# Hybrid conv and gMLP trunk on 8 cores: the 31-tap convolution over eight phases and 16 channels in place of four and 32

## The chip, the cores and the metric

The kernel runs on the 8 cores of one Trainium2 chip. Each core computes its own two sequences of 2048 tokens (4096 rows of 1024 channels); nothing passes between cores. The metric is the device time of one execution, in microseconds (us), of the slowest core.

## What is computed

Layer 0 is a convolution mixer and a squared-ReLU MLP, layer 1 a gMLP mixer and another MLP, with an RMSNorm ahead of each part and at the end. The change is in layer 0's mixer A and around it:

```python
z = h @ w_in  # (B, S, IN_EVEN)
a_val, a_gate, b_gate, c_gate, b_val = jnp.split(
    z, [A_DIM, 2 * A_DIM, 2 * A_DIM + B_DIM, 2 * A_DIM + 2 * B_DIM], axis=-1)
# A: GLU -> causal depthwise conv (31) -> LayerNorm over channels -> swish
a = a_val * jax.nn.sigmoid(a_gate)
a = causal_depthwise_conv(a, conv_a_w) + conv_a_b
a = jax.nn.silu(layer_norm(a, ln_a_g, ln_a_b))
# B: B * conv3(C * h)
bo = b_gate * causal_depthwise_conv(c_gate * b_val, conv_b_w)
return jnp.concatenate([a, bo], axis=-1) @ w_out  # shared pointwise output projection
```

A_DIM and B_DIM are 512. The gMLP mixer (layer 1) ends in `y @ w_out`, whose order of tiles the change touches too.

## The kernel before

**Macro tiles.** A core's 4096 tokens are four macro tiles (`mt`) of 1024 tokens. Each passes through mixer 0 (`Mixer0`), MLP 0, mixer 1 (`mixer1`), MLP 1 and the final norm. In a macro tile, token blocks `tb` are 128 tokens, halves `hf` are 512. Big products are groups of 8 matmuls of 128x512 (`fm_group`, `tm_group`, line L550). Eight PSUM banks are handed out in turn (`next_bank`); a bank is written again only when its reader is done with it.

**Order.** There is no scheduler. The kernel is written out by hand in one order; every engine executes its own instructions in that order, and `Prog` puts a semaphore wait where data or a buffer needs it. So an instruction that waits holds all that stands behind it on its engine. SP issues the loads of `x`, the stores of `y` and the DMAs that move data between partitions; GpSimd (POOL) issues the weight loads (a ring of five 1 MB slots, `issue`, `issue_quarter`; in the prologue by quarters).

**The convolution.** Time is split into phases: position t of a 1024-token tile is in phase t mod 4. After the gate (`glu`, which writes `aP`), 32 DMAs (`to_x`, L717) bring the 512 channels into `X`, whose 128 partitions are 4 phases x 32 channels, with 16 channel groups of 256 columns and 8 columns of history. The depthwise convolution is then a banded 128x128 matrix for each of 9 column shifts: `conv(m, pr)` (L793) is 2 groups x 9 matmuls of 256 columns, and there are 8 calls for each macro tile, 32 in all. The scalar engine (ACT) evicts each group twice (with bias L802, squared L805); `sums` adds up for the LayerNorm over channels (DVE and POOL), `stat_mm` (L830) sums over partitions with one fp32 matmul of 512 columns (two passes on TensorE), `ln_var`, `ln_rstd`, `ln_norm` (L849) normalise on DVE, `silu` (L854) is on ACT, 16 DMAs (`to_mix`, L859) bring the result back to channels on partitions (`mixA`), and eight small copies on DVE (`reorder`, L864) put it in the order of tokens in `mixTA`. `out` is the output projection; its first four groups (7 of 8 matmuls each) need the reorders of half 0 and branch B without its last quarter.

**Branch B** (`b_branch`): two products and a gate multiply for each half (`b_cv`), five tap operations on DVE (`b_taps`), two more products and multiplies (`b_gates`): 6 groups of 8 matmuls for each of 4 channel quarters m.

**Where it lies.** For macro tiles 2 and 3 the projections and branch B run ahead (`ahead`) before MLP 1 of the tile before, and the convolution, LayerNorm and `to_mix` are hung into that MLP (`behind`: keys (quarter of the MLP, 0 for the first product or 1 for the second, place in it)). Macro tile 1 uses `behind` too. Macro tile 0 has no such cover: its mixer is in the prologue, interleaved with the `glu` and branch B of tile 1 (`m1`). There, `stat_mm` of tile 0 stands in the fifth pair of `m1.glu`, the silus and `to_mix` in branch B quarters 0 and 1, the reorders of half 0 ahead of the taps of quarter 3, then `out` of tile 0. The norm of tile 1's input (`pre`: `load` by SP, `stat` on ACT and then two small POOL operations, `xn` on ACT, `tr` on TensorE and DVE) is also interleaved.

**Names in the trace.** Buffers of the arena (`X`, `aP`, `a_conv`, `mixA`, `cw` and others) all show as `arena`.

## Time and profile before

| | us |
|---|---|
| median of 3 runs | 2687.58 |
| lowest and highest run | 2686.13, 3231.77 |
| the profiled execution, its own time | 2687.07 |
| its span (slowest core, core 0) | 2685.5 |
| span of the fastest core (core 1) | 2673.3 |
| TensorE busy (core 0) | 2638.5 (98%) |
| VectorE, ScalarE, GpSimd busy | 1035.9, 879.4, 942.3 |

The median and the profiled execution belong to the same level; the highest run stands apart and nothing is compared with it. Engines are called PE (TensorE matmul), PEld (its weight loads), DVE (VectorE), ACT (ScalarE), POOL (GpSimd) and SP (the queue that issues DMAs). A row of the trace over time gives start, duration, engine, source line, operation, tiles, count, and in brackets the idle time ahead of it with what ended it. Since a PE row's duration includes the tail of its last matmul, the pace of matmuls is read from one row's start to the next row's start.

### The profile page before, as it was taken

Reading aid. Unit: us, or ns where it says so; the run is one execution under the profiler, and the core shown is the slowest. Engines: PE = TensorE matmul, PEld = TensorE weight load, DVE = VectorE, ACT = ScalarE, POOL = GpSimd, SP = SyncE. Lnnn points to the kernel's source line nnn. Section 1 sums busy time; section 2 is a strip of 40 time slices with the busy share of each in tenths; the row PEclk is TensorE's granted clock in tenths of the full one; section 3 lists DMA queues with packets and bytes.
Section 4 is the critical chain, followed back from the end, with each engine's and each line's share of the span. In section 5 each row is a group of like instructions: output and inputs, shape, how many; then the busy total and the mean of one; then the engine's idle time right before and its main releaser. Section 6 shows DMA issues by size and latency. Waiting matters only on the chain.

```text
span 2685.5 us, 39687 instructions; the slowest of 8 cores (2673.3 to 2685.5 us)
## 1 busy us (share of the span) xinstructions
PE 2638.5 (98%) x13400; PEld 1260.9 (47%) x13400; DVE 1035.9 (39%) x1582; ACT 879.4 (33%) x1487; POOL 942.3 (35%) x1229
## 2 busy tenths in 40 slices
PE   6999999999999999999999999999999999999998
PEld 3544444455444444445544444444554444444443
DVE  3564223732543115743245212655233512273223
ACT  2433115432333235412234223632223421354112
POOL 3214223333433342403453434142344333325223
PEclk9999999999999999999999999999999999999999
DMA  9426334455575533345558544155455834325432
GB/s 203 113 55 117 73 66 77 77 100 98 95 184 130 118 72 64 66 95 96 101 116 227 95 95 88 39 95 104 87 101 107 213 68 92 64 44 101 77 63 79
DMA packets 57908, 265.28 MB, mean 99 GB/s; under 512 B 8176, under 2 KB 16368, under 8 KB 33904
## 3 DMA queue, kind: packets, MB, share of 16 engines
q0 software_dynamic: 29664, 202.39, 42.0%
q1 hardware_dynamic: 28048, 60.37, 7.1%
q8 instruction: 112, 1.84, 0.3%
q14 instruction: 84, 0.69, 0.1%
HBM read 439.67 MB, written 17.04 MB: 170 GB/s over the span
## 4 chain that ended last, share of the span: by engine, by line
PE 95%; DMA 3%; DVE 1%; issue 1%; POOL 0%; ACT 0%; DVEq 0%; SPq 0%; POOLq 0%; ACTq 0%
PE bank L550 90%; PE bank L793 2%; PE bank L431 2%; DMA ring<-od_w_out 2%; DMA h<-x 0%; DMA arena<-x 0%; DVE arena L1022 0%; PE bank L1016 0%; DVE arena L970 0%; ACT junk L406 0%; PE bank L830 0%; DVE st L986 0%; DVE xnT L434 0%; DVE arena L995 0%; DMA y<-arena 0%
## 5 line engine op out<-in xcount | busy, mean ns | idle before, releaser
L550 PE MATMUL bank<-xnT,ring 128*128 128x512 bf16 x5888 | 1297.4, 380 | 9.5 <-ACT arena L634 5.8
L550 PE MATMUL bank<-ring,arena 128*128 128x512 bf16 x5120 | 1125.2, 379 | 5.4 <-DMA ring<-od_w_out 5.4
L572 DVE TENSOR_TENSOR h<-bank,h 128x512 f32<-128x512 f32 x640 | 440.7, 691 | 1303.8 <-PE bank L550 1263.2
L550 PEld LDWEIGHTS bank<-xnT,ring 128*128 128x128 bf16 x5888 | 574.2, 98 | 689.1 <-issue 21.9
L550 PEld LDWEIGHTS bank<-ring,arena 128*128 128x128 bf16 x5120 | 498.6, 98 | 594.2 <-issue 9.4
L600 POOL TENSOR_TENSOR arena<-arena 128x512 bf16<-128x512 f32 x512 | 551.4, 1083 | 313.8 <-ACT arena L598 313.6
L598 ACT ACTIVATE arena<-bank 128x512 f32<-128x512 f32 x512 | 303.7, 597 | 974.5 <-PE bank L550 930.5
L351 POOL DMA_DIRECT2D ring<-w x128 | 72.5, 567 | 453.7 <-PE bank L550 452.7
L406 ACT ACTIVATE junk<-h 128x1024 bf16<-128x1024 f32 x135 | 142.0, 1052 | 197.0 <-DVE h L572 178.8
L434 DVE TENSOR_TENSOR xnT<-bank,sm 128x1024 bf16<-128x1024 bf16 x128 | 155.2, 1217 | 50.6 <-PE bank L431 50.4
L408 POOL TENSOR_SCALAR st<-st 128x1 f32<-128x1 f32 x159 | 36.0, 227 | 372.2 <-ACT junk L406 370.3
L416 ACT ACTIVATE xn_tm<-h,st 128x1024 bf16<-128x1024 f32 x96 | 109.5, 1147 | 103.2 <-POOL st L410 103.2
L550 PE MATMUL bank<-ring,xnT 128*128 128x512 bf16 x512 | 115.7, 379 | 0.0
L410 POOL TENSOR_TENSOR st<-st,mhalf 128x1 f32<-128x1 f32 x159 | 92.6, 582 | 23.6 <-POOL st L408 0.3
L813 POOL TENSOR_TENSOR arena<-arena 128x512 f32<-128x512 f32 x16 | 20.3, 1268 | 224.1 <-ACT arena L805 224.1
L634 ACT ACTIVATE arena<-bank 128x512 f32<-128x512 f32 x64 | 38.1, 597 | 181.0 <-PE bank L550 148.6
L802 ACT ACTIVATE arena<-bank,sm 128x256 f32<-128x256 f32 x64 | 30.4, 474 | 201.2 <-PE bank L793 194.5
L635 DVE TENSOR_TENSOR arena<-bank,arena 128x512 bf16<-128x512 f32 (+1 forms) x64 | 44.2, 691 | 131.4 <-PE bank L550 100.6
L1022 DVE SCALAR_TENSOR_TENSOR arena<-bank,sm,biasT 128x128 f32<-128x128 f32 x256 | 86.0, 349 | 20.4 <-DVE arena L1022 0.5
L431 PE MATMUL bank<-ident,xn_tm 128*128 128x128 bf16 x896 | 68.9, 222 | 18.7 <-DVE xn_tm L1115 18.7
L431 PEld LDWEIGHTS bank<-ident,xn_tm 128*128 128x128 bf16 x896 | 59.8, 99 | 43.4 <-issue 19.5
L550 PEld LDWEIGHTS bank<-ring,xnT 128*128 128x128 bf16 x512 | 49.9, 98 | 59.5
(82 smaller groups left out, 1000.0 us busy)
## 6 DMA issues: line engine op xcount, KB each, us to landing
ring<-w POOLq DMA_DIRECT2D x128, 1024.0 KB, 10.4
arena<-convw POOLq DMA_DIRECT2D x16, 1152.0 KB, 11.9
h<-x SPq DMA_DIRECT2D x32, 512.0 KB, 6.7
ring<-od_w_in POOLq DMA_DIRECT2D x16, 1024.0 KB, 9.0
y<-arena SPq DMA_DIRECT2D x31, 512.0 KB, 4.3
arena<-x SPq DMA_DIRECT2D x24, 512.0 KB, 10.4
ring<-ev_w_in POOLq DMA_DIRECT2D x10, 1024.0 KB, 14.3
ring<-ev_w_out POOLq DMA_DIRECT2D x8, 1024.0 KB, 12.2
```

The costliest lines, as they stand in the source:

```text
L351: op("pool", lambda e: e.dma_start(out=ring[s][:], in_=W[wn][c]), [], wkeys(s), dma=f"w{s}")
L406: op("act", lambda e: e.activation(out=junk[:], in_=src, func=AF.Square, scale=1.0 / 32, accum_out=scol(c)), keys, [("st", c), ("junk",)])
L410: op("pool", lambda e: e.tensor_tensor(out=scol(c), in0=scol(c), in1=mhalf[:], op=ALU.pow), [("st", c), ("mhalf",)], [("st", c)])
L416: op("act", lambda e: e.activation(out=dst, in_=src, func=AF.Copy, scale=scol(c)), keys + [("st", c)], [dkey])
L431: r = e.transpose(tbk[:, kc * 128:(kc + 1) * 128], xa[:, kc * 128:(kc + 1) * 128], ident[:])
L434: op("dve", lambda e: e.tensor_tensor(out=xnT[:, :, tb * 128:(tb + 1) * 128], in0=tbk.rearrange("p (k n) -> p k n", k=8), in1=sm[:, SM_G + ...
L550: r = e.matmul(banks[b][:], lhsT=lhs(kc), rhs=rhs(kc), start=start and n == 0, stop=stop and n == len(kcs) - 1)
L572: op("dve", lambda e: e.tensor_tensor(out=h[:, tb, d * 512:(d + 1) * 512], in0=banks[b][:], in1=h[:, tb, d * 512:(d + 1) * 512], op=ALU.ad ...
L598: op("act", lambda e, b=b, rb=rb: e.activation(out=rbuf[rb], in_=banks[b][:], func=AF.Relu), [("ps", b)], [(f"rbuf{rb}",)])
L600: op("pool", lambda e, rb=rb, c=j * 4 + m, s=s, hq=hq: e.tensor_tensor(out=hq[:, c, s * 512:(s + 1) * 512], in0=rbuf[rb], in1=rbuf[rb], op ...
L793: r = e.matmul(banks[b][:, gi * 256:(gi + 1) * 256], lhsT=cw[wk][:, i, q, :], rhs=self.X[:, 4 * m + i, q:q + 256], start=(q == 0), stop=(q ...
L1022: op("dve", lambda e, b=b, j=j, g=g: e.scalar_tensor_tensor(out=svb[k][:, g, :], in0=banks[b][:, j * 128:(j + 1) * 128], scalar=sm[:, SM_L ...
```

## The change

It has these parts.

1. Eight phases of 16 channels: position t is in phase t mod 8. `X` has 32 groups of 128 columns with 4 columns of history, the band needs 5 shifts, and a `conv(c, pr)` call is 4 groups x 5 matmuls of 128 columns. `c` runs over four chunks of 8 groups. Weights of the convolution are 128 x 5120 for each chunk in place of 128 x 4608. Each call is evicted by 8 ACT operations of 128 columns in place of 4 of 256.
2. `to_x` is 4 x 16 DMAs in place of 2 x 16, `to_mix` 4 x 16 in place of 16, each over 16 partitions in place of 32. The reorders wait for all of `to_mix`.
3. `stat_mm` multiplies 256 columns in place of 512; `sums` folds on DVE and POOL.
4. `behind`: statistics, silus and `to_mix` earlier in the MLP (in quarter 2's first product, chunk by chunk), the reorders later.
5. `mixer1`: the output projection takes output half 0 of token blocks 0 to 2 first, then half 1 of them.
6. Prologue of tile 0: the first weight quarters are issued after the first statistic, blocks 4 and 5 are normalised earlier, four loads of tile 1's input come in the glu; `to_x` follows the glu; two of its chunks are issued after branch B quarter 1; `conv` of chunk 1 comes after branch B quarter 2; the statistics of `pre` for blocks 4 to 7 stand in `last_b` as pairs with their `xn`; `stat_mm` comes two glu pairs later; the silus and `to_mix` come within quarter 0 of tile 1's branch B; all eight reorders come after branch B.

The core of the diff (layout of the arena, packing of the inputs on the host and the same slicing in branch B are left out):

```diff
-            def to_x(self, pr):
+            def to_x(self, c):
+
                 def move(e, k):
-                    i, s = k // 4, k % 4
-                    return e.dma_start(
-                        out=self.X[32 * s:32 * s + 32].rearrange("p (m i) n -> p m i n", i=4)[:, 2 * pr:2 * pr + 2, i, 8:264],
-                        in_=aP[32 * i:32 * i + 32, 2 * pr:2 * pr + 2, s, :])
-                op("sp", move, [("aP", m, hf) for m in (2 * pr, 2 * pr + 1) for hf in range(2)], [(self.kX, pr)],
-                   dma=f"X{pr}", n=16)
+                    i, p = 2 * c + k // 8, k % 8
+                    return e.dma_start(out=self.X[16 * p:16 * p + 16, 4 * i:4 * i + 4, 4:132],
+                                       in_=aP[16 * i:16 * i + 16, :, p, :])
+                op("sp", move, [("aP", m, hf) for m in range(4) for hf in range(2)], [(self.kX, c)], dma=f"X{c}", n=16)
...
-            def conv(self, m, pr):
-                wk = m % 2 if self.mt == 0 else 0
...
+            def conv(self, c, pr):
...
+                wk = c % 2 if self.mt == 0 else 0
...
                 def go(e):
-                    for gi in range(2):
-                        i = pr * 2 + gi
-                        for q in range(9):
-                            r = e.matmul(banks[b][:, gi * 256:(gi + 1) * 256], lhsT=cw[wk][:, i, q, :],
-                                         rhs=self.X[:, 4 * m + i, q:q + 256], start=(q == 0), stop=(q == 8))
+                    for gi in range(4):
+                        for q in range(5):
+                            r = e.matmul(banks[b][:, gi * 128:(gi + 1) * 128], lhsT=cw[wk][:, 4 * pr + gi, q, :],
+                                         rhs=self.X[:, 8 * c + 4 * pr + gi, q:q + 128], start=(q == 0), stop=(q == 4))
                     return r
...
-                op("pe", lambda e: e.matmul(banks[b][:], lhsT=blk[:], rhs=part, start=True, stop=True),
-                   [("part", 0), ("part", 1), ("blk",)], [("ps", b)])
+                op("pe", lambda e: e.matmul(banks[b][:, 0:256], lhsT=blk[:], rhs=part_b, start=True, stop=True),
+                   [("part", "b", 0), ("part", "b", 1), ("blk",)], [("ps", b)])
...
-            def to_mix(self):
-                op("sp", lambda e, k: e.dma_start(out=mixA[32 * (k // 4):32 * (k // 4) + 32, k % 4],
-                                                  in_=self.sgate[32 * (k % 4):32 * (k % 4) + 32, k // 4]),
-                   [(self.kS, g) for g in range(16)], [("mixA",)], dma="mx", n=16)
+                    out=self.sgate[:, g, :], in_=a_conv[:, g, :], func=AF.Silu, bias=sm[:, SM_LNB + g:SM_LNB + g + 1],
+                    scale=sm[:, SM_LNG + g:SM_LNG + g + 1]), [ak(g), ("sm",)], [(self.kS, g)])
+
+            def to_mix(self, c):
+                def move(e, k):
+                    i, p = 2 * c + k // 8, k % 8
+                    return e.dma_start(out=self.mixA[16 * i:16 * i + 16, p], in_=self.sgate[16 * p:16 * p + 16, 4 * i:4 * i + 4, :])
+                op("sp", move, [(self.kS, g) for g in range(8 * c, 8 * c + 8)], [(self.kM, c)], dma=f"mx{c}", n=16)
 
...
-                    in_=half_cols(mixA[:, :, m], hf)), [("mixA",)], [(self.kA, m, hf)])
+                    out=self.mixTA[:, m, hf * 512:(hf + 1) * 512].rearrange("p (b s n) -> p s b n", b=4, s=8),
+                    in_=half_cols(self.mixA[:, :, m], hf)), [(self.kM, c) for c in range(4)], [(self.kA, m, hf)])
...
                 for t in range(4, 8):
+                    if t in late:
+                        nm.stat(t)
                     nm.xn(t)
...
-                self.glu({5: [lambda: self.to_x(0)], 7: [lambda: self.to_x(1)]})
+                self.x_halo()
+                self.glu()
+                for c in range(4):
+                    self.to_x(c)
...
-                self.save_halo()
+                side.setdefault((0, 0, 10), []).append(self.save_halo)
...
-                for m in range(4):
-                    fq, t0 = m // 2, (0, 6)[m % 2]
-                    add((fq, 1, t0), self.conv, m, 0)
-                    add((fq, 1, t0 + 1), self.conv, m, 1)
-                    if m < 3:
-                        add((fq, 1, t0 + 1), load_cw, self.mt, m + 1)
-                add((2, 0, 4), self.stat_mm)
-                add((2, 0, 4), self.ln_var)
-                add((2, 0, 6), self.ln_rstd)
-                for m in range(4):
-                    add((2, 0, 7 + 2 * m), self.ln_norm, m)
-                for g in range(16):
-                    add((2, 1, g // 2), self.silu, g)
-                add((2, 1, 7), self.to_mix)
+                for c, (k0, k1) in enumerate((((0, 1, 0), (0, 1, 1)), ((0, 1, 6), (0, 1, 7)),
+                                              ((1, 0, 12), (1, 0, 13)), ((1, 1, 4), (1, 1, 5)))):
+                    add(k0, self.conv, c, 0)
+                    add(k1, self.conv, c, 1)
+                    if c < 3:
+                        add(k1, load_cw, self.mt, c + 1)
+                add((2, 0, 1), self.stat_mm)
+                add((2, 0, 1), self.ln_var)
+                add((2, 0, 2), self.ln_rstd)
+                for c in range(4):
+                    add((2, 0, 3 + 3 * c), self.ln_norm, c)
+                    for i in range(8):
+                        add((2, 0, min(16, 5 + 3 * c + i // 4)), self.silu, 8 * c + i)
+                    add((2, 0, min(16, 6 + 3 * c)), self.to_mix, c)
                 for m in range(4):
                     for hf in range(2):
-                        add((3, 0, 6 + 2 * m + hf), self.reorder, m, hf, "dve")
+                        add((3, 0, 10 + m + hf), self.reorder, m, hf, "dve")
...
-            for tb in range(NTB):
-                for d in range(2):
...
-                post(tb)
+            order = [(tb, d) for d in range(2) for tb in range(3)] + [(tb, d) for tb in range(3, NTB) for d in range(2)]
+            for tb, d in order:
...
+                if d == 1:
+                    post(tb)
...
-        more_weights(2)
...
-        for tb in range(4, NTB):
-            load_h(0, tb, [("w", 0, 0), ("w", 1, 0)])
...
-            if tb < 3:
-                more_weights(2)
+            more_weights(2)
+            if tb == 0:
...
-        nm.stat(4)
-        first_xn(4)
+        for tb in (4, 5):
+            nm.stat(tb)
+            first_xn(tb)
         more_weights(3)
...
-        m0.glu({2: [lambda: pre.load(0, [("aP", 2, 0)]), lambda: pre.load(1)],
-                5: [lambda: m0.to_x(0)], 7: [lambda: m0.to_x(1)]})
-        prologue_spatial()
...
+        m0.glu({0: [first_tr(4), more_x(6, 3, 0)], 1: [first_tr(5), more_x(7, 3, 1)],
+                2: [first_tr(6), lambda: more_weights(3), lambda: [pre.load(t, [("aP", 2, 0)] if t == 0 else ()) for t in range(4)]],
+                5: [prologue_spatial]},
+               {3: [first_tr(7)]})
+        m0.x_halo()
+        m0.to_x(0)
+        m0.to_x(1)
...
-            pre.load(tb + 4)
+        for tb in (2, 3):
+            pre.stat(tb)
+            pre.xn(tb)
+        for tb in range(4, 8):
+            pre.load(tb)
+        m0.to_x(2)
+        m0.to_x(3)
         prologue_bias()
         m0.conv(0, 0)
...
+        m0.b_branch(2)
         m0.conv(1, 0)
         m0.conv(1, 1)
         load_cw(0, 3)
...
-        m0.b_branch(2)
-        for tb in (2, 3, 4, 5):
-            pre.stat(tb)
-        for tb in (2, 3):
...
+        rest = m0.last_b(pre, (4, 5, 6, 7))
         m1.weights(m0)
         m1.glu({0: [rest[0], lambda: m0.conv(2, 0)], 1: rest[1:] + [lambda: m0.conv(2, 1)],
-                2: [lambda: m0.conv(3, 0)], 3: [lambda: m0.conv(3, 1)],
-                4: [m0.stat_mm, m0.ln_var], 5: [m0.ln_rstd, lambda: m0.ln_norm(0)],
-                6: [lambda: m0.ln_norm(1)], 7: [lambda: m0.ln_norm(2)]})
+                3: [lambda: m0.conv(3, 0)], 4: [lambda: m0.conv(3, 1), m0.save_halo],
+                6: [m0.stat_mm, m0.ln_var], 7: [m0.ln_rstd, lambda: m0.ln_norm(0)]})
...
+        m0.ln_norm(1)
         m1.b_halo(0)
         m1.b_cv(0, 0)
         silus(0)
+        m0.ln_norm(2)
         m1.b_cv(0, 1)
         silus(1)
         m1.b_taps(0)
+        m0.ln_norm(3)
+        silus(2)
         m1.b_gates(0)
-        m0.ln_norm(3)
-        m1.b_halo(1)
-        m1.b_cv(1, 0)
-        silus(2)
-        m1.b_cv(1, 1)
         silus(3)
...
-        m0.to_mix()
-        for pr in range(2):
-            m1.to_x(pr)
-        m1.b_taps(1)
-        m1.b_gates(1)
+        for c in range(4):
+            m0.to_mix(c)
+        for c in range(4):
+            m1.to_x(c)
+        m1.x_halo()
+        m1.b_branch(1)
...
-        for m in range(4):
-            m0.reorder(m, 0, "dve")
         m1.b_taps(3)
         m1.b_gates(3)
         m1.free_in()
         for m in range(4):
-            m0.reorder(m, 1, "dve")
+            for hf in range(2):
+                m0.reorder(m, hf, "dve")
```

How this moves instructions, at the three places that matter later. First SP, at the end of the prologue (L859 before and L878 after are `to_mix` of tile 0, L717 and L728 are `to_x` of tile 1, L1227 and L1237 the load of `b_v`). Before:

```order
L859 DMA arena<-arena 32x1024 [waits s_act_0,s_dve_0]
L859 DMA arena<-arena 32x1024 x15
L717 DMA arena<-arena 32x2x256 [waits d_cb_0,s_pe_0]
L717 DMA arena<-arena 32x2x256 x31
L1227 DMA arena<-bigc 128x1024 [waits d_mx_0,d_mx_1,s_dve_0]
```

After:

```order
L878 DMA arena<-arena 16x512 [waits s_act_0,s_dve_0]
L878 DMA arena<-arena 16x512 x31
L878 DMA arena<-arena 16x512 [waits s_act_0]
L878 DMA arena<-arena 16x512 x15
L878 DMA arena<-arena 16x512 [waits s_act_0]
L878 DMA arena<-arena 16x512 x15
L728 DMA arena<-arena 16x4x128 [waits d_cb_0,s_pe_0]
L728 DMA arena<-arena 16x4x128 x63
```

Tile 0's way back is 64 DMAs on this queue where it was 16, each with half the partitions and half the elements of a partition; the first 32 of them wait for the silus of the first two chunks (the 32 share one wait).

Second DVE, at the end of tile 1's branch B (L864 and L882 are `reorder`, L755 to L759 and L764 to L768 the taps of quarter 3, L768 and L777 the last multiplies, L572 and L577 the sum into `h` behind `out`'s matmuls). Before:

```order
L635 TENSOR_TENSOR arena<-bank3,arena 128x4x128 [waits s_pe_0,s_act_0,s_pool_0]
L864 COPY arena<-arena 128x4x4x32 [waits d_mx_0,d_mx_1,d_cw1_0]
L864 COPY arena<-arena 128x4x4x32 x3
L755 TENSOR_SCALAR arena<-arena,sm 128x1024 [waits s_pool_0,s_dve_0]
...
L768 TENSOR_TENSOR arena<-bank4,arena 128x4x4x32 [waits s_pe_0,s_dve_0]
L768 TENSOR_TENSOR arena<-bank5,arena 128x4x4x32 [waits s_pe_0]
L864 COPY arena<-arena 128x4x4x32 x4
L572 TENSOR_TENSOR h<-bank6,h 128x512 [waits s_pe_0]
```

After:

```order
L640 TENSOR_TENSOR arena<-bank3,arena 128x8x64 [waits s_pe_0,s_act_0,s_pool_0]
L764 TENSOR_SCALAR arena<-arena,sm 128x1024 [waits s_pool_0,s_dve_0]
...
L777 TENSOR_TENSOR arena<-bank4,arena 128x8x4x16 [waits s_pe_0,s_dve_0]
L777 TENSOR_TENSOR arena<-bank5,arena 128x8x4x16 [waits s_pe_0]
L882 COPY arena<-arena 128x8x4x16 [waits d_mx0_0,d_mx0_1,d_mx1_0,d_mx1_1,d_mx2_0,d_mx2_1,d_mx3_0,d_mx3_1,d_cw1_0]
L882 COPY arena<-arena 128x8x4x16 x7
L577 TENSOR_TENSOR h<-bank6,h 128x512 [waits s_pe_0]
```

The four copies of half 0 that stood ahead of the taps now stand behind the last multiplies, with the wait for all four chunks of `to_mix`.

Third ACT, around `last_b` of tile 0 (L406 and L411 are `stat`, L416 and L421 `xn`, L634 and L639 the evictions of gates). Before:

```order
L406 ACTIVATE junk,st<-arena 128x1024 [waits d_st2_0,s_act_0]
L406 ACTIVATE junk,st<-arena 128x1024 [waits d_st3_0,s_act_0]
L634 ACTIVATE arena<-bank0 128x512 [waits s_pe_0,s_dve_0]
L634 ACTIVATE arena<-bank5 128x512 [waits s_pe_0,s_dve_0]
L416 ACTIVATE xn_tm0<-arena,st 128x1024 [waits s_pool_0]
L416 ACTIVATE xn_tm1<-arena,st 128x1024 [waits s_pool_0]
L416 ACTIVATE xn_tm2<-arena,st 128x1024 [waits s_pool_0,s_pe_0]
L416 ACTIVATE xn_tm3<-arena,st 128x1024 [waits s_pool_0,s_pe_0]
```

After:

```order
L639 ACTIVATE arena<-bank0 128x512 [waits s_pe_0,s_act_0,s_dve_0]
L639 ACTIVATE arena<-bank5 128x512 [waits s_pe_0,s_act_0,s_dve_0]
L411 ACTIVATE junk,st<-arena 128x1024 [waits d_st0_0]
L421 ACTIVATE xn_tm0<-arena,st 128x1024 [waits s_pool_0]
L411 ACTIVATE junk,st<-arena 128x1024 [waits d_st1_0,s_act_0]
L421 ACTIVATE xn_tm1<-arena,st 128x1024 [waits s_pool_0]
L411 ACTIVATE junk,st<-arena 128x1024 [waits d_st2_0,s_act_0]
L421 ACTIVATE xn_tm2<-arena,st 128x1024 [waits s_pool_0,s_pe_0]
```

The statistics that waited for loads ahead of the two gate evictions now stand behind them, each followed by the `xn` that needs POOL's answer to it.

## Rows read from the trace of the kernel before

**Rows 1.** The page, busy time, share of the span and instructions: PE.

```profile
PE 2638.5 (98%) x13400; PEld 1260.9 (47%) x13400; DVE 1035.9 (39%) x1582; ACT 879.4 (33%) x1487; POOL 942.3 (35%) x1229
```

**Rows 2.** Instructions over time, PE, a convolution call between two products.

```profile
582.20 2.14 PE L793 MATMUL bank<-arena 128*128 128x256 bf16 x18
584.17 3.62 PE L550 MATMUL bank<-ring,arena 128*128 128x512 bf16 x16
```

**Rows 3.** The same view: sixteen transposes of 128 columns.

```profile
106.41 1.06 PE L431 MATMUL bank<-ident,xn_tm 128*128 128x128 bf16 x16
107.30 1.89 PE L550 MATMUL bank<-xnT,ring 128*128 128x512 bf16 x8
```

**Rows 4.** Groups by line and form, PEld: busy us, mean ns, idle before.

```profile
L793 PEld LDWEIGHTS bank<-arena 128*128 128x128 bf16 x576 | 55.8, 97 | 12.2
```

**Rows 5.** Instructions over time, PE: the statistics' matmul and what follows.

```profile
150.52 1.10 PE L830 MATMUL bank<-arena,blk 128*128 128x512 f32 x2 [1.50 <-POOL arena L819]
151.45 51.96 PE L550 MATMUL bank<-xnT,ring 128*128 128x512 bf16 x240
```

**Rows 6.** PE over time: waits at mixer 1's output projection.

```profile
521.65 12.25 PE L550 MATMUL bank<-ring,arena 128*128 128x512 bf16 x56 [1.90 <-DMA ring<-od_w_out]
...
1105.93 1.89 PE L550 MATMUL bank<-ring,arena 128*128 128x512 bf16 x8 [0.66 <-DMA ring<-od_w_out]
...
1762.92 1.89 PE L550 MATMUL bank<-ring,arena 128*128 128x512 bf16 x8 [0.73 <-DMA ring<-od_w_out]
...
2421.26 13.93 PE L550 MATMUL bank<-ring,arena 128*128 128x512 bf16 x56 [2.09 <-DMA ring<-od_w_out]
```

**Rows 7.** Spans and granted clock of the cores.

```profile
core 0: 2685.5 us, clock 0.996
core 1: 2673.3 us, clock 0.997
```

**Rows 8.** PE over time in the prologue: waits for inputs and for ACT.

```profile
23.74 9.66 PE L550 MATMUL bank<-xnT,ring 128*128 128x512 bf16 x32 [1.48 <-DVE xnT L434]
...
44.98 36.38 PE L550 MATMUL bank<-xnT,ring 128*128 128x512 bf16 x160 [2.25 <-DVE xnT L434]
...
115.84 9.69 PE L550 MATMUL bank<-xnT,ring 128*128 128x512 bf16 x32 [5.76 <-ACT arena L634]
```

**Rows 9.** All engines over time, 100 to 117 us: ACT and POOL there.

```profile
111.74 1.06 ACT L406 ACTIVATE junk<-arena 128x1024 bf16<-128x1024 f32 x1 [7.76 <-DMA arena<-x]
...
115.03 0.19 ACT L406 ACTIVATION_READ_ACCUMULATOR junk<-arena 128x1 f32 x1
115.12 1.06 ACT L634 ACTIVATE arena<-bank 128x512 f32<-128x512 f32 x2
...
115.74 0.57 POOL L410 TENSOR_TENSOR st<-st,mhalf 128x1 f32<-128x1 f32 x1
...
116.08 1.15 ACT L416 ACTIVATE xn_tm<-arena,st 128x1024 bf16<-128x1024 f32 x1
```

**Rows 10.** The issues on SP's queue over time: start, us for all.

```profile
54.67 23.80 SPq L717 DMA_DIRECT2D arena<-arena  x32
...
80.86 1.73 SPq L650 DMA_DIRECT2D wsT_bf<-ws_scr  x4
...
180.41 10.06 SPq L859 DMA_DIRECT2D arena<-arena  x16
190.62 21.99 SPq L717 DMA_DIRECT2D arena<-arena  x32
```

**Rows 11.** DMA issues, 150 to 212 us: size, median us to landing.

```profile
arena<-arena SPq DMA_DIRECT2D x16, 64.0 KB, 2.0
```

**Rows 12.** All engines over time, 150 to 222 us: silus, reorders, `out`.

```profile
168.28 2.06 ACT L854 ACTIVATE arena<-arena,sm 128x256 bf16<-128x256 f32 x4
...
200.82 0.89 DVE L864 COPY arena<-arena 128x512 bf16<-128x512 bf16 x4
...
203.25 13.98 PE L550 MATMUL bank<-ring,arena 128*128 128x512 bf16 x64
...
205.90 1.29 DVE L768 TENSOR_TENSOR arena<-bank,arena 128x512 bf16<-128x512 f32 x2
```

286 lines of the change are left out of this document (141 added, 145 removed).

## The prediction

> **What bounds the kernel now.** I read the page first. PE is busy 98% of the span [rows 1], so time is won only by fewer PE columns or by removing PE waits; a faster DVE, ACT or POOL is worth nothing where PE does not wait for it. Then PE over time: from about 150 us on it runs in one piece, with four short waits for the output weights of mixer 1 [rows 6]. All other PE idle time lies in the prologue (tile 0), where there is no MLP to hide anything [rows 5, 8]. So there are two questions: what PE work goes, and what the new order does to PE's waits in the prologue. The pace of a full product: 240 matmuls of 512 columns start at 151.45 and the next piece at 203.25 [rows 5, 12], 51.8 / 240 = 0.216 us each, 1.727 us for a group of 8.
>
> **The convolution.** A call of 18 matmuls of 256 columns takes 584.17 - 582.20 = 1.97 us [rows 2]. The new call has 20 matmuls of 128 columns. The nearest row with that shape and a new weight load for each matmul is the transposes: 16 in 107.30 - 106.41 = 0.89 us, 0.0556 us each [rows 3]. So 20 x 0.0556 = 1.11 us, 0.86 us less, and 32 calls give 27.5 us. Bounds: a weight load shows 97 ns for one [rows 4]; if each of the 20 were paid in full, a call would be 1.94 us and nothing would be won. The 16 transposes have the same loads and speak against it, so I take 0.0556.
>
> The Trainium skill (TensorE: Matmul & The Clock Gate, Back-to-back issue gap) gives about 81 ns as the sustained spacing of 128-column matmuls with weight loads. The row shows 55.6 ns over 16 of them; by the page a call would be 1.62 us and the 32 calls would give 11.2 us.
>
> **Smaller PE terms.** The statistics' matmul takes 151.45 - 150.52 = 0.93 us [rows 5]; half the columns, half of that, four times: 1.9 us. The 1.50 us that PE waited ahead of it in tile 0 [rows 5] goes, since a second glu pair (3.45 us) now stands between the last convolution and it: 1.5 us.
>
> **Mixer 1's output weights.** PE waits 1.90 + 0.66 + 0.73 + 2.09 = 5.4 us for the second of two weight tiles [rows 6]. The new order does two more groups (3.45 us) of the first tile before it needs the second; each wait is shorter than that. The fourth wait was also followed by a slower stretch: the same 56 matmuls take 13.93 in place of 12.25 us [rows 6], 1.7 us. Together 7.1 us. These waits are those of core 0; the fastest core ends 12.2 us earlier [rows 7], so the slowest cores gain here and come nearer to the others.
>
> **Start of the prologue.** PE's losses that show: waits of 1.48 and 2.25 us, and slow stretches after them (32 matmuls in 9.69 us where 32 x 0.216 plus a tail of 0.16 is 7.1; 160 in 36.38 where it would be 34.7) [rows 8], 8 us together. The first weight quarters now leave DMA room for the first inputs, but themselves come later, and blocks 4 to 7 have to wait for them. The same bytes have to arrive, so I count a little under half: 3.5 us won. Bounds: 8 us won; 5 us lost if the quarters come late by most of the time they are now issued later.
>
> **Around `last_b`.** Before, ACT waited 7.76 us for a staged load, with gate evictions behind it [rows 9]; PE lost 5.76 us and then 2.6 us in a slow stretch [rows 8]. The loads are now early, and the evictions stand ahead. But the four statistics now each have their `xn` right behind: 1.06 + 0.19 us, then POOL's answer about 1.1 us later (115.22 to 116.31), then 1.15 us [rows 9]: 3.5 us a pair, 14 us for four, and the first gate eviction of `m1.glu` is queued behind them. Counted from `last_b`'s start, ACT is free of them at about 22.4 us and evicts by 23.0; PE comes to the bank again at about 20.5. So 2.5 us of waiting, some 4 us more while DVE (taps, multiplies, transposes) catches up, and 2.6 us of slow clock: about what goes. I count 0. Bounds: 8.4 us won, 4 us lost.
>
> **The way back of tile 0.** This is where the change costs. Count from the end of the statistics' matmul. PE now has one glu pair and 24 groups of branch B before `out`: 26 x 1.727 = 44.9 us (before 30 groups, 51.8). The first `to_mix` waits for the first half of the silus; before, that half ended at 168.28 + 2.06 = 170.3 [rows 12], 18.9 us after the statistics [rows 5]. The chain of table loads and normalisation is the same and two pairs fewer lie in between: I take 17. SP then issues 64 DMAs. A `to_mix` DMA costs SP 10.06 / 16 = 0.63 us, and `to_x` 21.99 / 32 = 0.69 us, with half the bytes and twice the pieces [rows 10]: the price is for one DMA, not for its size. So 64 x 0.63 = 40.3 us, the last lands 2.0 us later [rows 11]: 59.3. The reorders wait for all of it, and `out` needs seven of the eight at 0.89 / 4 = 0.22 us [rows 12]: 60.9. PE waits 60.9 - 44.9 = 16.0 us, and after such a wait pays a slow stretch as above, 2.6 us: 18.6 us lost. Before, half of the reorders were done at 201.7, ahead of `out` at 203.25 [rows 12], with only 16 DMAs. Lower bound: even with all data there, the reorders now stand behind the last multiplies, which end at 207.19 less the 0.89 of the copies that moved, 3.1 us after PE gets to `out`, plus 1.6: 4.6 us. Upper bound: 19 us to the silus and 23.80 / 32 = 0.74 us a DMA, as when weights stream beside it [rows 10]: 27.7 us.
>
> **Hidden.** In tiles 1 to 3 the same 64 and 64 DMAs have room: `to_x` 64 x 0.69 = 44 us against branch B and MLP product of over 69 us (40 groups) ahead of the first convolution; `to_mix` 40 us against 36 groups (62 us) between the first chunk and the reorders. The doubled count of evictions (8 of 128 columns for 4 of 256) is on ACT, whose share is 33% [rows 1], under products; if that cover failed, 64 more operations of some 0.25 us a tile would be 16 us.
>
> **Sum.** 27.5 + 1.9 + 1.5 + 7.1 + 3.5 = 41.5 us won, 18.6 lost: 22.9 us. The profiled execution's span is 2685.5 us, so 2662.6; its own time is 2687.07, half a microsecond under the median of 2687.58, so the median would be 2664.7: I say **2665**.
>
> **The rivals.**
> - A, SP is quicker with half-width DMAs. The four DMAs into `wsT_bf` took 1.73 / 4 = 0.43 us each [rows 10]. Then `to_mix` is in time and only the lower bound of 4.6 us remains: 41.5 - 4.6 = 36.9, so 2651. For it: that row. Against: those have DRAM on one side, the two kinds from SBUF to SBUF cost 0.63 and 0.69.
> - B, the prologue's start wins nothing and loses 3 us, because the first weights come later: 2671. For it: the first product needs two quarters which are now issued behind the first statistic.
> - C, weight loads bound the short matmuls at 81 ns: 16.3 us less won, 2681. Against it: rows 3. The Trainium skill's page above is the source of that spacing; no row here shows it.
> - D, the other side: SP's issue slows to 1.2 us, since each DMA has smaller pieces and the weight loads of `out` and MLP 0 compete. The wait at `out` is 17 + 64p + 3.6 - 44.9, with 2.6 of clock 64p - 21.7; at p = 1.2 it is 55.1 us, net 13.6 lost, 2701. It decides from p = 0.99 us on. Against it: 0.74 us is the slowest row [rows 10].
> - E, everything goes well (A, `last_b` and the start at their bounds): 2687.6 - 36.9 - 8.4 - 4.5 = 2638.
>
> **How the numbers follow.** Forecast 0.48, A 0.22, B 0.13, C 0.07, D 0.05, E 0.05. The range reaches from A to B with some room for their own terms: 2646 to 2677, leaving out C, D and E. A difference of 2% (54 us) is about what a measurement of this kernel can tell from no change: faster than 2634 needs more than E, 0.03; slower than 2741 needs D and more, 0.02; within 2%, 0.95.
>
> **What would show it.** A convolution call between two products takes 1.11 us. PE shows one wait of some 16 us at `out` of tile 0, ended by the reorders, and these waited for a DMA; SP's 64 issues take 40 us. No wait for `od_w_out`. PE's first product starts earlier than 23.7 us. A wait of 2 to 3 us, ended by ACT's gate eviction, follows `last_b`. The forecast is wrong if a call takes 1.6 us or more, if SP takes 0.45 us or 1 us a DMA, or if new waits show in tiles 1 to 3.

## The result and the profile after

The forecast was 2665 us in a range of 2646 to 2677. Measured were 2705.5 us (2705.75 and 2705.27) against 2687.58: 1.007 of the time before, 95% interval 1.0041 to 1.01. So the change costs some 0.7% where 0.8% was to be won. The forecast, its range and its sign are wrong; "within 2%" holds. Every time given here and below is a median of those executions in which no four cores of the chip were slowed down together by a much lower granted clock.

Cores 0 and 1 took 2685.5 and 2673.3 us before [rows 7]; they and all others are later now, and core 6 ends 9 to 19 us behind cores 0 to 5.

The kernel after, spans and mean granted clock of the cores:

```profile
core 0: 2693.8 us, clock 0.989
core 1: 2688.8 us, clock 0.990
...
core 5: 2684.8 us, clock 0.990
core 6: 2704.1 us, clock 0.981
core 7: 2696.4 us, clock 0.982
```

I compare core 0 with core 0, since the rows before are of that core, and come back to cores 6 and 7 below. The kernel after, PE over time on core 0 (start us, busy us, ..., in brackets the idle time ahead of the row and what ended it):

```profile
19.22 5.00 PE L555 MATMUL bank<-xnT,ring 128*128 128x512 bf16 x16 [1.48 <-DVE xnT L439]
29.66 1.01 PE L436 MATMUL bank<-ident,xn_tm 128*128 128x128 bf16 x8 [5.45 <-DVE xn_tm L1133]
...
77.60 1.95 PE L666 MATMUL bank<-arena 128*128 128x128 f32 x16
88.74 4.42 PE L801 MATMUL bank<-arena 128*128 128x128 bf16 x40 [9.19 <-DMA arena<-arena]
92.96 10.91 PE L555 MATMUL bank<-xnT,ring 128*128 128x512 bf16 x48
108.66 4.43 PE L801 MATMUL bank<-arena 128*128 128x128 bf16 x40 [4.80 <-DMA arena<-arena]
112.88 6.00 PE L555 MATMUL bank<-xnT,ring 128*128 128x512 bf16 x24
118.72 1.06 PE L436 MATMUL bank<-ident,xn_tm 128*128 128x128 bf16 x16
...
129.59 1.29 PE L801 MATMUL bank<-arena 128*128 128x128 bf16 x20
130.72 3.62 PE L555 MATMUL bank<-xnT,ring 128*128 128x512 bf16 x16
138.53 1.01 PE L436 MATMUL bank<-ident,xn_tm 128*128 128x128 bf16 x8 [4.20 <-ACT arena L639]
140.23 2.29 PE L801 MATMUL bank<-arena 128*128 128x128 bf16 x20 [0.69 <-DVE arena L640]
...
166.24 0.59 PE L847 MATMUL bank<-arena,blk 128*128 128x256 f32 x2
166.67 45.06 PE L555 MATMUL bank<-xnT,ring 128*128 128x512 bf16 x208
237.52 15.43 PE L555 MATMUL bank<-ring,arena 128*128 128x512 bf16 x64 [25.79 <-DVE arena L882]
```

The first bracket with a DMA is new and stood nowhere in the prediction: PE waits 9.19 and 4.80 us for X ahead of convolution chunks 0 and 1. The last is the forecast wait at `out`, but 25.79 us long and not 16. Behind 237.52 PE has one wait left on this core, 1.37 us at 617.39 for convolution weights, and none on the others. (A call of the convolution is the row at 129.59; the transposes at 118.72 are those of `last_b`.) The core's way, cut at the same points of the program in both kernels, with the terms of the prediction put at their places. (The kernel before: the first cut is the row of the 16 bias matmuls below, the others are in [rows 3, 5, 12]; the spans are in [rows 7] and above.)

```profile
81.20 1.95 PE L661 MATMUL bank<-arena 128*128 128x128 f32 x16
```

| piece of core 0 | before | after | change | forecast |
|---|---|---|---|---|
| to the bias matmuls | 81.20 | 77.60 | -3.6 | -3.5 |
| to the transposes in `last_b` | 25.21 | 41.12 | +15.9 | -3.4 |
| to the statistics' matmul | 44.11 | 47.52 | +3.4 | +2.0 |
| to `out` | 52.73 | 71.28 | +18.6 | +8.6 |
| `out` to the end | 2482.3 | 2456.3 | -26.0 | -26.5 |
| sum | | | +8.3 | -22.8 |

The forecast column is worked out thus: 4 calls of the convolution at 0.86 in each of the second and third piece; in the third also two glu pairs more ahead of the statistics (6.9) and the wait of 1.5 that goes; in the fourth 60.9 - 51.8 and half a microsecond of statistics; in the last 24 calls (20.6), three statistics (1.4), 7.1 for the output weights, less the 2.6 of slow clock behind the wait. Three pieces came out within 1.5 us. Two did not, and they are 29.3 of the 31.1 us by which this core missed its forecast: 19.3 us for X and 10.0 us at `out`. In the 19.3 us are 14.0 of waiting; most of the rest is the slow stretch behind each wait (40 matmuls in 4.2 us, row start to row start, for 2.3).

**The wait for X.** The kernel after, SP's queue over time on core 0:

```profile
40.21 3.63 SPq L392 DMA_DIRECT2D arena<-x  x4
45.64 0.33 SPq L654 DMA_DIRECT2D ws_scr<-arena  x1
71.65 4.98 SPq L655 DMA_DIRECT2D wsT_bf<-ws_scr  x8
76.73 21.18 SPq L728 DMA_DIRECT2D arena<-arena  x32
98.07 3.40 SPq L392 DMA_DIRECT2D arena<-x  x4
101.51 27.25 SPq L728 DMA_DIRECT2D arena<-arena  x32
```

Before, `to_x` stood ahead of the `ws_scr` store and was issued from 54.67 on [rows 10]. Now the store is ahead, and the loads of `wsT_bf` wait until it has landed, 26 us after its issue. The store's issue in the kernel before, then its DMA row (size, median us to landing) before and after:

```profile
78.58 0.53 SPq L649 DMA_DIRECT2D ws_scr<-arena  x1
```

```profile
ws_scr<-arena SPq DMA_DIRECT2D x1, 256.0 KB, 2.2
```

```profile
ws_scr<-arena SPq DMA_DIRECT2D x1, 256.0 KB, 25.9
```

It came into a time in which staged inputs, convolution weights and input weights fill the DMA engines (share 1.01 to 1.06 from 40 to 72 us; before, 0.33 around 80 us). So `to_x` starts 22 us later, and the convolution behind it waits.

**The wait at `out`.** SP's 64 issues of `to_mix` take from 184.64 to 226.15, 0.65 us each (forecast 0.63), and start 18.0 us after the statistics (forecast 17). But the reorders begin at 235.87, not two microseconds after the last issue. The kernel after, core 0 by windows (PE, PEld, DVE, ACT, POOL busy; granted clock; DMA share; GB/s):

```profile
180.00:211.00 31.00, 31.00 (x146) 14.09 (x144) 24.77 (x34) 14.14 (x34) 5.35 (x10) 1.00 0.23 50
211.00:218.00 7.00, 0.73 (x4) 0.12 (x2) 3.47 (x6) 0.00 (x0) 0.75 (x2) 0.90 0.81 126
218.00:225.00 7.00, 0.00 (x0) 0.00 (x0) 0.00 (x0) 0.00 (x0) 0.00 (x0) 0.50 1.03 161
225.00:236.00 11.00, 0.00 (x0) 0.00 (x0) 0.13 (x1) 0.00 (x0) 0.00 (x0) 0.50 0.96 158
```

From 211 us on the DMA engines are nearly full (share 0.81, then 1.03 and 0.96). POOL issues three weight tiles of 1 MB there:

```profile
210.16 1.06 POOL L356 DMA_DIRECT2D ring<-w  x2
212.27 0.53 POOL L356 DMA_DIRECT2D ring<-w  x1 [1.05 <-PE bank L555]
```

They are released when branch B gives up its input weights, which is now in the midst of the 64 transfers. The `to_mix` transfers behind them take 12.0 us (median) from issue to landing between 211 and 218, and 1.8 between 195 and 211. The DMA rows of the two stretches, 195 to 211 first:

```profile
arena<-arena SPq DMA_DIRECT2D x26, 16.0 KB, 1.8
```

```profile
arena<-arena SPq DMA_DIRECT2D x11, 16.0 KB, 12.0
```

**Cores 6 and 7.** The kernel after, core 6, 160 to 210 us:

```profile
160.00:210.00 50.00, 49.59 (x211) 21.66 (x209) 30.83 (x40) 26.07 (x61) 8.54 (x13) 0.81 0.25 51
```

Core 6 is granted 0.81 from 100 to 261 us where it does not wait, core 7 likewise; cores 0 to 5 have 1.00 from 160 to 210 us. What that costs is seen on the 208 matmuls behind the statistics, 45.06 us on core 0 (above). PE over time on core 6:

```profile
175.32 54.79 PE L555 MATMUL bank<-xnT,ring 128*128 128x512 bf16 x208
247.29 14.90 PE L555 MATMUL bank<-ring,arena 128*128 128x512 bf16 x52 [17.19 <-DVE arena L882]
```

These take 9.7 us longer, and nearly all of it is hidden, since PE then waits 17.19 us at `out` and not 25.79. Core 6 sets the time, 10.3 us behind core 0. Of these 10.3 us, 2.0 are there already at the bias matmuls (79.64 against 77.60), ahead of the lower clock, and 1.9 are a longer wait for X. The other 6 or so go with the lower clock. In the second of the two runs cores 4 and 5 had it (mean clock 0.981 and 0.980) and ended 9 us behind the rest.

### The profile page after: what moved, and what is told of

Same layout as the page of the kernel before. It is cut to its first block, busy times and chain, and to the rows that moved or that the text cites. A ratio compares the mean times of both kernels' runs of the same rounds, so it can differ in the third digit from the quotient of the medians.

```text
span 2704.1 us, 40449 instructions; the slowest of 8 cores (2684.8 to 2704.1 us)
## 1 busy us (share of the span) xinstructions
PE 2634.1 (97%) x13464; PEld 1251.5 (46%) x13464; DVE 1029.9 (38%) x1553; ACT 911.2 (34%) x1679; POOL 946.3 (35%) x1224
## 4 chain that ended last, share of the span: by engine, by line
PE 92%; DMA 3%; SPq 2%; POOL 1%; issue 1%; ACT 1%; DVE 0%; DVEq 0%; POOLq 0%; ACTq 0%
PE bank L555 88%; PE bank L436 2%; SPq L878 1%; PE bank L801 1%; DMA ws_scr<-arena 1%; DMA arena<-arena 1%; SPq L728 1%; DMA h<-x 1%; PE bank L1034 1%; POOL ring L361 0%; DMA ring<-ev_w_in 0%; ACT arena L871 0%; ACT junk L411 0%; POOL st L415 0%; SPq L655 0%
## 5 line engine op out<-in xcount | busy, mean ns | idle before, releaser
L555 PE MATMUL bank<-xnT,ring 128*128 128x512 bf16 x5888 | 1315.6, 384 | 1.9 <-DVE xnT L439 1.9
L577 DVE TENSOR_TENSOR h<-bank,h 128x512 f32<-128x512 f32 x640 | 439.3, 691 | 1191.9 <-PE bank L555 1150.9
L411 ACT ACTIVATE junk<-h 128x1024 bf16<-128x1024 f32 x135 | 141.9, 1051 | 223.4 <-DVE h L577 200.3
L421 ACT ACTIVATE xn_tm<-h,st 128x1024 bf16<-128x1024 f32 x96 | 109.5, 1147 | 101.0 <-POOL st L415 94.8
L810 ACT ACTIVATE arena<-bank,sm 128x128 f32<-128x128 f32 x128 | 49.0, 383 | 167.3 <-PE bank L801 167.3
L639 ACT ACTIVATE arena<-bank 128x512 f32<-128x512 f32 x64 | 38.2, 599 | 181.4 <-PE bank L555 145.0
L436 PE MATMUL bank<-ident,xn_tm 128*128 128x128 bf16 x896 | 70.0, 224 | 21.9 <-DVE xn_tm L1133 19.8
L833 POOL TENSOR_TENSOR arena<-arena 128x512 f32<-128x512 f32 x24 | 33.4, 1390 | 161.3 <-ACT arena L813 160.7
## 6 DMA issues: line engine op xcount, KB each, us to landing
ring<-w POOLq DMA_DIRECT2D x128, 1024.0 KB, 10.3
```

The costliest lines, as they stand in the source:

```text
L411: op("act", lambda e: e.activation(out=junk[:], in_=src, func=AF.Square, scale=1.0 / 32, accum_out=scol(c)), keys, [("st", c), ("junk",)])
L421: op("act", lambda e: e.activation(out=dst, in_=src, func=AF.Copy, scale=scol(c)), keys + [("st", c)], [dkey])
L436: r = e.transpose(tbk[:, kc * 128:(kc + 1) * 128], xa[:, kc * 128:(kc + 1) * 128], ident[:])
L555: r = e.matmul(banks[b][:], lhsT=lhs(kc), rhs=rhs(kc), start=start and n == 0, stop=stop and n == len(kcs) - 1)
L577: op("dve", lambda e: e.tensor_tensor(out=h[:, tb, d * 512:(d + 1) * 512], in0=banks[b][:], in1=h[:, tb, d * 512:(d + 1) * 512], op=ALU.ad ...
L810: op("act", lambda e, g=g, src=src, bias=bias: e.activation(out=a_conv[:, g, :], in_=src, func=AF.Identity, bias=bias, scale=1.0), [("ps", ...
```

## The experiments

Ratios are to the kernel before on the same chip. Three chips were used, on which the kernel before took 2689.5 (experiments 1 to 4), 2687.7 (5, 6, 7 and 10) and 2692.1 us (8 and 9, where its runs spread from 2689 to 2709).

**1. SP's order.**

```
-        def prologue_spatial(): ... sp: ws_scr store, 8 loads of wsT_bf
+        def spatial_dma():      ... the same, called behind m0.to_x(1)
```

(Both lines are shortened, the dots stand for the calls.)

> The changed kernel, but SP issues the store to ws_scr and the eight loads of wsT_bf behind the first two to_x calls, as the kernel before did. Theory Q (SP's queue): the two waits for X ahead of convolution chunks 0 and 1 (9.19 and 4.80 us on core 0) come from SP standing until the ws_scr store lands (27.8 us). They vanish together with their slow stretches (2.7 and 3.0 us): 19.7 us of 2705.5, so 2686. Theory T (the transfers themselves are late, since stage loads, convolution weights and input weights fill the DMA engines between 40 and 75 us): to_x starts 18 us earlier but lands late, a wait of 3 to 6 us stays at chunk 0: 2695. Theory L on two cores' clock level of 0.812 from 100 to 261 us: if the level follows from the waits, it goes, and the slowest core gains some 10 us more: 2676.

2688.4 us, ratio 0.9993 (0.998 to 1.0007). The trace, core 0:

```profile
56.93 26.18 SPq L730 DMA_DIRECT2D arena<-arena  x32
...
82.34 4.02 PE L803 MATMUL bank<-arena 128*128 128x128 bf16 x40 [3.84 <-DMA arena<-arena]
```

Theory Q holds for most: `to_x` is issued 19.8 us earlier, and of 14.0 us of waiting for X 5.0 are left on core 0, 7.4 on core 6, 8.1 on core 3. The rest is theory T: sixteen transfers issued in 13 us from 56.93 on have landed by 82 only (14.4 us from issue to landing in the median, at a DMA share of about 1). Core 0 gained 13.4 us between the two traces; over all cores and runs it was 6 to 8 us (2683.1 on average; the kernel after in experiment 5, on another chip, 2691.5 over its four runs and 2689.1 over the two without lowered cores), not 19.7. What remains for X, waits of 1 to 3 us that PE's earlier arrival opens behind it, and a wait at `out` of 24.1 to 27.0 us, where cores 0 to 5 had 22.5 to 25.8, take the rest. Theory L can't be judged from this: no core's mean clock is under 0.987 here, but experiment 5 shows the level missing in half of the runs of the unchanged kernel too.

**2. The weights of MLP 0 held back.**

```
+        hold.append((m0.kM, 3))      # loads issued from here also wait for to_mix chunk 3
         m1.free_in()
+        hold.clear()
```

> The changed kernel, but the three 1 MB weight loads that POOL issues at 210 to 212 us, when branch B gives up its weights, also wait for the last to_mix transfer of tile 0. Theory D (these loads fill the DMA engines from 211 us on and the last 22 to_mix transfers stand behind them, 12 us from issue to landing in place of 1.8): the last lands 2 us after its issue at 226.1, the wait at out falls from 25.8 to 17.5 us on core 0: 2697. Theory S (the late landings are SP's own issue): no change, 2705. Price to watch: the loads come 17 us later, and MLP 0 begins 28 us after out; if they take over 25 us, PE waits for the ring.

2701.8 us, a single run, so without an interval. The trace, waits of core 0 (us in total, times, longest):

```profile
PE bank L556 <- DVE arena L883: 17.3, 1, 17.3
...
PE bank L556 <- ACT arena L604: 6.3, 1, 6.3
```

The wait at `out` is 17.3 us against 25.8, forecast 17.5: theory D. The transfers between 195 and 232 us now land 1.8 us after their issue (median). What was gained went into the wait at MLP 0 of 6.3 us, but not for the reason I had put down as its price. POOL, core 0:

```profile
286.24 0.29 POOL L734 COPY halo_x<-arena 128x128 bf16<-128x128 bf16 x1 [18.48 <-DMA arena<-arena]
```

PE waits for ACT's ReLU, ACT for POOL's squares, and these stand behind a halo copy that waits for the last `to_x` of m1, whose 64 issues end at 277. In the kernel after, they end at 270 and the copy runs at 274 without a wait. The held loads have a part in that: they now run beside these `to_x` (12.8 us from issue to landing between 226 and 250 us, for 2.4 in the kernel after), and the last 16 meet two more 1 MB loads issued at 266.6 (10.6 us for 1.9). So holding the loads moved the collision from `to_mix` to `to_x`.

**3. Two queues for `to_mix`.**

```
+                if self.mt or c % 2 == 0: op("sp", ...)
+                else:                     op("pool", ...)
```

> The changed kernel, but in tile 0 half of to_mix (chunks 1 and 3, 32 transfers) is issued by POOL. Theory P (the wait at out is the count of issues on one queue): if POOL takes 0.53 us each, as its weight loads do (1.06 us for 2), both queues are through 20 us after the silus; only the reorders behind the last multiplies are left, a wait of 5 in place of 25.8 us: 2685. Rival G: POOL needs over 1 us for a transfer in so many pieces, 32 of them take as long as SP's 64 did, and its halo copies stand behind: wait of 15 to 25 us at out and new waits in branch B: 2700 to 2715.

2686.3 us, ratio 0.9989 (0.9978 to 1.0). The trace, core 2, POOL over time and then PE's waits:

```profile
184.77 15.41 POOL L878 DMA_DIRECT2D arena<-arena  x32 [1.92 <-ACT arena L871]
```

```profile
PE bank L555 <- DVE arena L777: 5.3, 2, 4.9
PE bank L555 <- DVE arena L886: 4.7, 1, 4.7
```

Theory P: POOL takes 0.48 us a transfer, SP 0.63, and the wait at `out` is 4.7 us, which is the prediction's lower bound of 3.1 + 1.6 for reorders behind the last multiplies. Half of rival G came too: POOL's halo copy stands behind its 32 issues, and branch B waits 4.9 us.

**4. The four late statistics.**

```
+        for tb in range(4, 8):
+            pre.stat(tb)
-        rest = m0.last_b(pre, (4, 5, 6, 7))
+        rest = m0.last_b(pre)
```

> The changed kernel, but the four statistics of staged blocks 4 to 7 are taken in one go ahead of last_b, as before the change, and not each ahead of its xn. Theory E (the wait of 4.20 us after last_b, ended by ACT's gate eviction, is four statistics at 1.25 us and the way to POOL and back between statistic and xn, 3.5 us a pair): the wait of 4.20 + 0.69 us and the slow stretch of 2.7 us go: 2698. Rival M: the statistics only move, 5 us of them now stand ahead of the evictions of the last branch B block, and PE waits there: 2705.

2688.8 us, ratio 1.0003 (0.9993 to 1.0014). On core 0 the 4.20 and 0.69 us are gone, and nothing of that size is in their place (waits of 2.7 and 1.9 us for the gate eviction are left on cores 3 and 4): theory E. The means of the cores are 2680 to 2684, 7 to 9 us under those of experiment 5.

**5. The kernel after once more.**

> The changed kernel as it is, once more. In its first trace cores 6 and 7 had a granted clock of 0.812 from 100 to 261 us and ended 10 us behind the others; none of the undisturbed runs of the three variants with fewer waits showed such a level. Theory K (that level belongs to this kernel's pattern of waits): two of eight cores have it again, 2705. Theory R (it was an accident of those runs or that chip): all cores within 2682 to 2696, so 2697, and the variants' gains shrink by the same 8 us.

2700.85 us, ratio 1.0052 (1.0035 to 1.007). The waits are there again on this chip: 10.2 to 16.6 us for X and 22.9 to 24.9 us at `out` on cores 0, 2 and 6. Of four runs two took 2696.7 and 2697.3 with every core at 0.988 or more, as theory R has it. Two took 2704.4 and 2704.8, with cores 0 and 1 (in one of them 0 to 3) at a mean clock of 0.985 to 0.987; none fell to the 0.981 of core 6 above. In the 25 runs of experiments 1 to 4 no core's mean was under 0.987. So a lower clock on some cores came in 4 of 6 runs of this kernel and made 8 to 9 us of its time each time, but its form was not the same. It is not this kernel's alone, against theory K: on the last chip the kernel before had two cores at 0.986 and two at 0.988 in one run each (2708.8 and 2703.1 us), and cores 6 and 7 of experiment 9's kernel stood at 0.981 in one run. And 0.81 over some 8 to 12 us stands in the traces of experiments 2 and 3 on cores 0 to 3, of 8 on cores 6 and 7 and of 9 on cores 4 to 7. What triggers it stays open. Where it is absent, the change costs 9 us.

**6. The three edits together.** SP's order, the statistics and both queues of experiments 1, 4 and 3 in one kernel.

> The changed kernel with three edits together: SP's ws_scr store and wsT_bf loads behind the first two to_x; the four late statistics ahead of last_b in one go; half of tile 0's to_mix issued by POOL. Alone they took about 9, 8 and 10 us off the ordinary cores (2692 to 2683, 2684, 2682). Theory I (the waits are independent, since they stand at different places of one chain): they add up, ordinary cores at 2665, the time about 2670. Theory S (what is won ahead of out comes back as waiting at out or for the weights of MLP 0): 2680.

2670.8 us, ratio 0.9937 (0.9921 to 0.9954). Theory I: they add up, means of the cores 2660 to 2669, against 2685 to 2695 in experiment 5.

**7. The rest of the waits.**

```
-        m0.conv(0, 0) ...            ahead of m0.b_branch(2)
+        m0.conv(0, 0) ...            behind it
+        m1.b_halo(1)
+        m0.to_mix(3)                 on POOL, behind that halo copy
+        m0.reorder(m, hf, "dve")     all 8, between m1.b_cv(3, 1) and m1.b_taps(3)
```

> The three edits, and more: convolution chunk 0 behind branch B's block 2, so that its X has 10 us more to land; POOL issues chunk 3 of to_mix only behind the halo copy of m1's block 1 (which had kept PE 4.88 us); the eight reorders stand on DVE ahead of block 3's taps, not behind its multiplies. Theory I: of e5's waits the 5 us for X, 4.9 in branch B and 4.7 at out go, 2658. Rival B: to_mix lands after 212 us, DVE waits for it with the taps and multiplies of block 3 behind it, and out begins no sooner than in e5: 2668. Rival C: chunk 0's convolution in front of chunk 1's leaves too little time for the next convolution weights, a new wait of some 5 us ahead of chunk 2: 2663.

(Of the order of calls only what moves is shown; m1's `x_halo` moves up with `b_halo(1)`.) 2663.9 us from two runs, ratio 0.9911 (0.9891 to 0.9931). The trace, core 0, PE over time and then its waits:

```profile
149.03 45.93 PE L555 MATMUL bank<-xnT,ring 128*128 128x512 bf16 x208
194.79 13.98 PE L555 MATMUL bank<-ring,arena 128*128 128x512 bf16 x64
```

```profile
PE bank L555 <- ACT arena L603: 6.8, 1, 6.8
PE bank L555 <- ACT arena L639: 3.5, 1, 3.5
```

`out` begins without a wait, 43 us earlier than in the kernel after and 8.5 earlier than before. The waits of theory I are gone, but for at most 2.7 us for X, and there is no sign of rivals B and C. The time is 6 us above the forecast of theory I, since two waits are back: the one at MLP 0 of experiment 2, and 3.5 us after `last_b`, since two chunks' 32 evictions now stand in one piece ahead of the statistics.

**8. The halo copy behind MLP 0.**

```
-            if mt == 0:
-                m1.save_halo()       # ahead of mlp(0)
             mlp(0, norm_tail(2), side)
+            if mt == 0:
+                m1.save_halo()
```

> The last combination (chunks behind block 2, reorders ahead of block 3's taps and so on) with one more edit: POOL saves m1's halo behind MLP 0 and not ahead of it. That trace showed a wait of 6.8 us on core 0 (4.8 on core 5) at MLP 0, ended by ACT's ReLU; ACT waited 17.9 us for POOL's squares, and these stood behind the halo copy, which waited 18.1 us for the last to_x of m1. Theory H: the copy goes, so the wait goes with its slow stretch of 2.0 us: 2664 less 7 to 9, 2656. Rival W: the weights of MLP 0, loaded since 193 us, or the squares themselves hold PE there: 2662.

2665.5 us, ratio 0.9891 (0.9843 to 0.9938). The wait at MLP 0 is gone on all cores, and cores 0 to 3 have mean spans of 2645 to 2652 against 2679 to 2681 of the kernel before: 31 us. On this chip cores 4 to 7 had a lower granted clock in both kernels (0.990 to 0.992 and 0.993) and set both times. Theory H in the trace; in the time the chip hides it.

**9. Blocks 4 to 7 not held back.**

```
-                    load_h(0, t, [("w", 0, 0), ("w", 1, 0)])
+                    load_h(0, t)
```

> The same kernel, but the loads of row blocks 4 to 7 no longer wait for the first two weight quarters. Theory N (PE's wait of 4 to 6 us after its first 16 products is only the gate: these loads are issued 17 us after the first ones): the wait goes, 4 us won, 2652. Rival B (the DMA engines are what is short at the start): the first quarters land later by what blocks 4 to 7 take, the first product moves from 19.2 to 22 us or more, and nothing is won or up to 3 us lost: 2656 to 2659.

2673.8 us, ratio 0.9925 (0.9896 to 0.9955). The trace, core 0, PE:

```profile
22.10 6.35 PE L555 MATMUL bank<-xnT,ring 128*128 128x512 bf16 x16 [4.20 <-DMA ring<-ev_w_in]
```

Rival B: the 5 us of waiting for block 4 go, the first product comes at 22.1 and not 19.0, and cores 0 to 3 end as in experiment 8 (2648 against 2649). What is short there is DMA (its engines are 93% busy in the first 30 us), not the order. The 8 us by which the time lies above experiment 8 are on cores 4 to 7, at a mean clock of 0.987 to 0.991, and say nothing of the edit.

**10. The output order alone, in the kernel before.**

```
+            order = [(tb, d) for d in range(2) for tb in range(3)] + ...
```

> The kernel before, with one edit: mixer 1's output does the first three row blocks of weight tile 0 ahead of those of tile 1, as the changed kernel does. The prediction's term: the four waits for od_w_out (5.4 us) and the slow stretch behind the last (1.7 us) go: 7.1 us, ratio to before 0.9974. Rival O: the slowest core is another one without such long waits, or the wait moves to a later place: under 2 us, ratio 0.9993 or more.

2688.4 us, ratio 1.0002 (0.9993 to 1.0012). No core waits for `od_w_out` any more, and the time is the same: rival O, in part. In the trace of before only cores 0, 3, 4 and 7 have these waits at all (4.0 to 5.4 us). The two halves of the chip part ways. Of cores 4 to 7 the one that ends last ends at 2677.2 us in place of 2682.8 (mean over the runs): 5.6 us won, near the forecast. Of cores 0 to 3 it ends at 2686.6 in place of 2685.9, with the clock at 0.993 to 0.994 in place of 0.995 to 0.996, and this half sets the time. The lower clock stands in pieces of 5 to 10 us, some ten of them on core 0 between 520 and 2440 us. The experiment's kernel, core 0 and then core 4:

```profile
515.00:530.00 15.00, 15.00 (x79) 7.14 (x78) 11.30 (x30) 3.21 (x5) 14.54 (x14) 0.94 1.00 155
```

```profile
515.00:530.00 15.00, 14.89 (x75) 7.08 (x76) 10.48 (x27) 3.19 (x5) 14.00 (x15) 1.00 1.05 164
```

Whether less waiting brought the lower clock on, or this chip's cores 0 to 3 had it anyway, is open; the kernel before had less of it on the same chip (0.993 on cores 0 and 1 in three or four of its 13 runs).

## Why the prediction was wrong

Forecast and result lie 40.5 us apart. Some 31 of them are core 0's, nearly all at two steps: a wait in tile 0 that was priced at nothing (19.3 us, under "Hidden") and the landing of the last `to_mix` (most of 10.0 us, under "The way back"). The other 10 are core 6's, which ends behind core 0. The terms one by one:

- **Bound of the kernel**: right. PE is at 97%, and what moved was PE work and PE waits, in the prologue and at mixer 1's output.
- **The convolution**: right. A call takes 130.72 - 129.59 = 1.13 us, forecast 1.11 from the transposes. From `out` of tile 0 to the end the cores without waits for `od_w_out` (1, 2, 5, 6) took 2474.6 us before and 2455.3 to 2456.8 after, 18 to 19 less. In that are slow stretches behind the wait at `out` of 2.0 to 3.5 us on these cores, so 24 calls and three statistics gave 21.3 (forecast 22.0). Rival C, 81 ns a matmul, is out: by it the 24 calls would give 8.4 us. The Trainium skill's figure (TensorE: Matmul & The Clock Gate, Back-to-back issue gap) does not hold here: the trace shows 56 ns a matmul.
- **The start**: 3.6 us for 3.5 on core 0, so rival B is out there. That the size fits is in part luck: it was taken as a little under half of 8 us, and over the eight cores the gain is 0.3 to 5.3 us, 3.1 on average.
- **Around `last_b`**: right in sum. The wait is 4.20 + 0.69 us, ended by ACT's gate eviction, for 2.5 us forecast; the 4 us of DVE catching up are 1.9 in two waits. The piece came out 1.4 us longer than forecast.
- **Output weights**: the size was about right for the cores that had the waits, the step from there to the time was not. In experiment 10 the last of cores 4 to 7 gains 5.6 us, for 7.1 forecast; cores 0 to 3 run at a lower clock and keep the time where it was (ratio 1.0002, at most 2 us won).
- **"Hidden"**: this is the first step that failed, and 19.3 us were lost by it. Experiment 1 moves the store and the `wsT_bf` loads back, and 9 of the 14 us of waiting go. I looked at `to_x` in tiles 1 to 3, where it does hide, and not in tile 0; and I listed what `prologue_spatial` issues nowhere, though it is moved past `to_x` on SP's queue and holds a wait for its own store. Priced from the rows before it would have looked like nothing, because the store landed there in 2.2 us. It landed in 26 when issued among the prologue's loads.
- **The way back**: mechanism, issues (64 at 0.65), start of the transfers (18.0 for 17) and the reorders were right; the step "the last lands 2.0 us later" was not, and it is the second that failed. It took a landing time from a stretch in which nothing else was loaded, [rows 11], while the same program point now meets three 1 MB loads: 9.7 us from the last issue to the first reorder instead of 2.0. That is 7.7 of the 10.0 us; the rest is 1.2 in the issues and 1.0 in the start. With the loads held back (experiment 2) the wait is 17.3 us, near the 16.0 forecast. My upper bound of 27.7 us did hold the 27.2 measured (25.79 and 1.45 of slow clock), but the range was drawn around a wait of 16 us.
- **The slowest core**: nothing in the prediction allowed for two cores at a clock of 0.81. In experiment 5 the runs with lowered cores take 8 us more than those without; the level's cause stays open.
- **New waits in tiles 1 to 3**: one, 1.4 us for convolution weights, on core 0. This sign of being wrong is met by the letter and costs next to nothing.
- **The rivals**: none describes the outcome. D has its sign and nearly its time (2701), but by SP's pace, which was 0.65 and not 1.2.

## What to carry to other kernels

When a step is moved on a queue that issues DMAs, write down every wait on that queue between its old and its new place, and ask of each what the transfer it waits for shares the engines with at the new time; a landing time is a property of its moment. When the count of small transfers grows, their issue time can be forecast well from like rows, but look up which large loads are released within the longer stretch. And where one core stands for eight, compare the others before a wait is counted in full, and see at what clock the cores that set the time were running. From 2701 to 2664 us it then took only moved waits and a second queue, with the same arithmetic.
